# Weight loads reordered around the write of the rows, and the first expert pair's rows selected on TensorE from SBUF

## The reference

```python
h = h + hier_moe(rmsnorm(h))                       # 32 experts in 4 groups, 2 experts per token
h = h + sigmoid(rmsnorm(h) @ W_g) * (p @ W_p)      # "ple"

def hier_moe(t):
    # group by softmax, then the two best of its 8 experts; gates (token, 32), two of them not 0
    h1 = einsum('td,edf->tef', t, w_gate)          # 1024 -> 256, per expert
    h2 = einsum('td,edf->tef', t, w_up)
    a  = silu(h1) * h2 * gates[:, :, None]
    return einsum('tef,efd->td', a, w_down)        # 256 -> 1024, per expert
```

## Time and profile before

| | us |
|---|---|
| median of 3 runs | 1132.73 |
| lowest and highest run | 1126.98, 1135.36 |
| the profiled execution | 1129.97 |
| its span in the trace | 1128.3 |

### The profile page before, as it was taken

The page is one execution under the profiler, slowest core; times in us unless marked ns, Lnnn a source line. Parts: engine busy times, 40 slices in busy tenths (PEclk is TensorE's granted clock), DMA queues, the critical chain, the costliest instruction groups (busy, mean ns, idle before and its releaser), DMA issues.

```text
span 1128.3 us, 13602 instructions
## 1 busy us (share of the span) xinstructions
PE 1037.9 (92%) x5168; PEld 645.2 (57%) x5168; DVE 368.3 (33%) x941; ACT 191.1 (17%) x393; POOL 124.4 (11%) x170
## 2 busy tenths in 40 slices
PE   7999997999998788999999999999989999877893
PEld 5767665444433335777777777777654444333372
DVE  4555224222222013632236444221432222121154
ACT  2123123111111012221112010001211111111121
POOL 2443001111111101000000000000021111110101
PEclk9999998899999999999999999999969999999997
DMA  9956948699999978933334322343669999999511
GB/s 361 362 151 213 413 190 319 245 421 420 422 419 424 420 321 315 372 112 129 133 112 148 105 99 98 114 140 142 248 248 417 421 420 419 424 421 390 196 82 42
DMA packets 61475, 305.99 MB, mean 271 GB/s; under 512 B 13762, under 2 KB 21154, under 8 KB 29538
## 3 DMA queue, kind: packets, MB, share of 16 engines
q1 hardware_dynamic: 44064, 273.46, 60.8%
q0 software_dynamic: 14656, 25.72, 6.8%
q10 hardware_dynamic: 2690, 5.93, 1.4%
HBM read 308.10 MB, written 21.08 MB: 292 GB/s over the span
## 4 chain that ended last, share of the span: by engine, by line
PE 63%; DMA 22%; issue 7%; POOLq 3%; POOL 2%; DVE 2%; ACT 1%; SPq 0%; ACTq 0%; DVEq 0%
PE ps L1684 17%; DMA ring_sb<-stream 13%; PE ps L1536 13%; PE ps L1732 8%; PE ps L1545 6%; DMA scr_sb<-stream 5%; PE ps L1617 3%; PE ps L1446 3%; DMA hn_rows<-scr_sb 2%; PE ps L1522 2%; POOLq L486 2%; PE ps L1488 2%; DMA scr_sb<-hn_rows,scr_sb 1%; POOL ring_sb L487 1%; PE ps L1633 1%
## 5 line engine op out<-in xcount | busy, mean ns | idle before, releaser
L1684 PE MATMUL ps<-hn_sb,ring_sb 128*128 128x288 f32 x768 | 195.0, 408 | 0.0
L1536 PE MATMUL ps<-ring_sb,scr_sb 128*64 128x512 f32 x704 | 166.0, 621 | 26.3 <-DMA ring_sb<-stream 26.3
L1684 PEld LDWEIGHTS ps<-hn_sb,ring_sb 128*128 128x128 f32 x768 | 142.6, 190 | 37.3 <-DVE hn_sb L749 0.3
L1536 PEld LDWEIGHTS ps<-ring_sb,scr_sb 128*64 128x64 f32 x704 | 54.5, 143 | 133.9 <-issue 133.8
L1050 DVE SCALAR_TENSOR_TENSOR scr_sb<-ps,scr_sb 128x256 f32<-128x256 f32 x32 | 15.5, 484 | 254.7 <-ACT scr_sb L643 254.7
L1732 PE MATMUL ps<-scr_sb,ring_sb 128*128 128x288 f32 x384 | 95.3, 407 | 0.0
L1545 PE MATMUL ps<-ring_sb,scr_sb 128*64 128x512 f32 x352 | 85.5, 620 | 1.1 <-ACT scr_sb L647 0.9
L1732 PEld LDWEIGHTS ps<-scr_sb,ring_sb 128*128 128x128 f32 x384 | 72.2, 190 | 19.4
L1536 PE MATMUL ps<-scr_sb 128*64 128x512 f32 x240 | 73.0, 609 | 2.5 <-DMA scr_sb<-stream 2.5
L1617 PE MATMUL ps<-scr_sb,ring_sb 128*128 128x288 f32 x256 | 64.3, 406 | 0.0
L1138 DVE TENSOR_TENSOR scr_sb<-ps,std_rstd_sb 128x288 f32<-128x288 f32 x48 | 21.8, 453 | 124.4 <-PE ps L1684 124.4
(11 more groups left out here) (276 smaller groups left out, 1227.5 us busy)
## 6 DMA issues: line engine op xcount, KB each, us to landing
ring_sb<-stream SPq DMA_DIRECT2D x188, 1024.0 KB, 14.7
scr_sb<-stream SPq DMA_DIRECT2D x50, 1024.0 KB, 26.6
hn_sb<-stream SPq DMA_DIRECT2D x10, 1024.0 KB, 27.4
ring_sb<-row_pages POOLq DMA_DIRECT2D x64, 128.0 KB, 5.0
scr_sb<-key_pages SPq DMA_DIRECT2D x24, 192.0 KB, 9.1
ring_sb<-key_pages SPq DMA_DIRECT2D x24, 192.0 KB, 5.8
scr_sb<-y_rows POOLq DMA_DIRECT2D x8, 512.0 KB, 6.1
hn_rows<-scr_sb ACTq DMA_DIRECT2D x4, 512.0 KB, 10.0
```

The source lines that it names most:

```text
L1536: last = mm(ps[64 * a:64 * a + 64, 2 + b, :], xT[:, k, 64 * a:64 * a + 64], slot(a + 2 * (k // 4))[:, (k % 4) * 512:(k % 4) * 512 + 512], ...
L1684: last = mm(bank((i + 1) % 4, T), ring(s, (i % 2) * D + k * P, P), hn_t[:, k, :], start=(k == 0), stop=(k == KD - 1))
```

## The change

1. The side places are taken by the slots with n mod 18 in 8, 9, 10, 15, 16, 17. So the loads to places 12 to 14 are issued after the eighth slot of the layer, before four further loads to the ring, and not after the twelfth.
2. The load to place 15 (n = 15) waits until the rows have been written (`hn_rows`). The load to place 16 (n = 16) waits until the first pair's rows have been selected (`x_ps`, 1) and the gather of pair 1 has landed (`x_got_1`, 16). The one to place 17 waits for `member` and `rank_ps`, as before.
3. Pair 0 is not gathered. VectorE makes `m01` for pair 0 with `both(0)` right after the first `members`, and TensorE computes the transposed rows as products of `hn_tok` with `m01`: 8 column blocks x 3 token tiles, into the same PSUM banks. A float32 product is two instructions, so they are 48; they take the place of the eight transposes of `x_turn(0)`.
4. On TensorE `keep_busy(0, 1)` is gone, and `project(6, KD)` stands in its place, ahead of the first `list_pair`. `list_pair(2)` stands behind the products, `list_pair(3)` behind the first `gate_up`, and `list_pair(4)` behind the first `a_turn`.
5. On VectorE `copy_x(1)` comes before the second `take_list`; the third list goes behind `times_up` of pair 0, and the rows of the tail (`row_tail`, eight small instructions) behind `times_up` of pair 4.

```diff
+SIDE_AT = [8, 9, 10, 15, 16, 17]
...
     for L in range(2):
-        for n in range(RING, 90):
-            if n % 18 >= RING:
-                side[S_PROJ[L] + n] = n % 18
+        for n in range(90):
+            if n % 18 in SIDE_AT:
+                side[S_PROJ[L] + n] = RING + SIDE_AT.index(n % 18)
...
-        for s in range(RING, 2 * RING):
+        for s in range(RING, N_SLOTS):
             if s == RING + ROW_POS[5]:
                 sp.wait_ge(sem("rows_free"), 8)
-            load_slot(s)
-        for s in range(2 * RING, N_SLOTS):
             for L in range(2):
-                if s == S_PROJ[L] + 12:
+                if s == S_PROJ[L] + SIDE_AT[0]:
                     if L == 0:
                         sp.wait_ge(sem("key_free"), 8)
                     else:
                         sp.wait_ge(sem("g_sb"), FT)
                         sp.wait_ge(sem("vs_ps"), 1)
-                if s == S_PROJ[L] + 15:
-                    sp.wait_ge(sem("hr_ps"), 2 * L + 2)
-                if s == S_PROJ[L] + 16:
+                if s == S_PROJ[L] + SIDE_AT[3]:
                     sp.wait_ge(sem("hn_rows"), 48 * (L + 1))
+                if s == S_PROJ[L] + SIDE_AT[4]:
+                    sp.wait_ge(sem(f"x_ps{L}"), 1)
+                    sp.wait_ge(sem(f"x_got{L}_1"), 16)
+                if s == S_PROJ[L] + SIDE_AT[5]:
                     sp.wait_ge(sem(f"member{L}"), 1)
                     sp.wait_ge(sem("rank_ps"), 2 * L + 2)
...
-            for c in range(3):
+            for c in range(1, 3):
                 gather(c)
...
             members(0)
+            both(0)
             take_list(slots[:, 0, :], gr[:, 0, :], 1)
+            dve.wait_ge(sem("m01"), 2 * L + 1)
             members(1)
-            take_list(slots[:, 1, :], gr[:, 1, :], 2)
-            members(2)
             dve.wait_ge(sem("rank_ps"), 2 * L + 2)
             link(nc.vector.tensor_reduce(cmx, ps[:, 6, 0:32], AX.X, ALU.max))
             nc.vector.tensor_copy(cnt_i[:, L:L + 1], cmx).then_inc(sem("cnt"), 1)
+            copy_x(1)
+            take_list(slots[:, 1, :], gr[:, 1, :], 2)
+            members(2)
...
-            copy_x(1)
-            take_list(slots[:, 2, :], gr[:, 2, :], 3)
-            members(3)
...
             for n in range(PAIRS):
                 times_up(n + 1, n % 2, gr[:, n, :])
+                if n == 0:
+                    take_list(slots[:, 2, :], gr[:, 2, :], 3)
+                    members(3)
...
-            keep_busy(0, 1)
+            project(6, KD)
+            pe.drain().then_inc(sem("slot_free"), 1)
 
             pe.wait_ge(sem("sel_tv"), 4 * L + 4)
             list_pair(1, None)
-            project(6, 7)
+            pe.wait_ge(sem("m01"), 2 * L + 1)
+            for k in range(KD):
+                for t, (t0, tn) in enumerate(TOK):
+                    last = mm(ps[:, k // 4, (k % 4) * P:(k % 4) * P + P], hn_tok[0:tn, t, k * P:k * P + P], m01[0:tn, t, :],
+                              start=(t == 0), stop=(t == 2))
+            last.then_inc(sem(f"x_ps{L}"), 1)
             list_pair(2, 1)
-            project(7, KD)
-            pe.drain().then_inc(sem("slot_free"), 1)
             pe.wait_ge(sem("prj"), 8 * L + KD)
...
-            pe.wait_ge(sem(f"x_got{L}_0"), 16)
-            x_turn(0)
-            list_pair(3, 2)
             for n in range(PAIRS):
...
                 last.then_inc(sem(f"h_ps{L}"), 1)
+                if n == 0:
+                    list_pair(3, 2)
                 if n + 1 < PAIRS:
-                    pe.wait_ge(sem(f"x_got{L}_{(n + 1) % 2}"), 16 * ((n + 1) // 2 + 1))
+                    pe.wait_ge(sem(f"x_got{L}_{(n + 1) % 2}"), 16 * (n // 2 + 1))
                     x_turn((n + 1) % 2)
...
                 a_turn()
-                if n + 3 < PAIRS:
+                if n == 0:
+                    list_pair(4, 3)
+                elif n + 3 < PAIRS:
                     list_part(2, 5).then_inc(sem(f"list_ps{L}"), 1)
```

23 lines of the change are left out of this document (12 added, 11 removed).

## The result

| | before | after |
|---|---|---|
| median of 20 runs each | 1131.76 | 1137.03 |
| lowest and highest run | 1126.98, 1135.36 | 1129.63, 1143.92 |
| the profiled execution | 1129.97 | 1135.79 |
| its span in the trace | 1128.3 | 1134.1 |

The ratio of after to before is 1.0052, with a 95% interval of 1.0034 to 1.0071: the change makes the kernel slower by 0.5%. The time lies in the stated range, and the case "within 1%" came true, but the forecast was 0.7 us faster (1132 against the 1132.73 of then), and the kernel is 5.3 us slower. The difference of the two spans, 5.8 us, is what has to be found in the trace.

The account below looks back on a forecast made before the run. The gapless weight stream was taken to bound the expert parts. Full clock gave -2.4 - 0.6 + 1.0 = -2.0 us, partly low clock +1.6; taken -0.5 on 1132.73, forecast 1132 us, range 1124 to 1143.

Parts of the forecast that it names:

- within 1%: Whole kernel: the time differs from before by no more than about 1%, chance 0.76.
- The end of the expert part is the time from which the stream runs without a gap, plus all that is left to move: Expert parts of both layers: an earlier TensorE start helps only as much as the gapless weight loads restart earlier.
- The stream starts again with n = 16 and not with n = 19 ... even at 202.5 and 830.5: SP's loads, both layers: three more slots, 7.5 us, remain; predicted restart at 200.1 and 829.9 gains 2.4 and 0.6 us.
- I take the middle of the two near cases: TensorE's clock: between not falling (-2.0 us) and low for a part (+1.6), taken as -0.5 us.
- for a part of the products: TensorE's products: 14 of 48 at low clock, 1.3 us per layer, slower first list in layer 1; sum +1.6 us.
- low throughout: First rival, TensorE's products: half clock makes them 11.6 to 14.6 us, kernel 1142 to 1148 us; chance 0.2.
- 48 x 0.152 = 7.3 us: TensorE's products for pair 0: 48 instructions at 0.152 us each, priced from row L1707, take 7.3 us per layer.
- the full-clock case: Clock not falling during the products: restart gains of 2.4 and 0.6 us less 1.0 for gather 2, -2.0 us.
- The other reordered lists ... TensorE is ahead of the stream there: 0: Moved lists and `row_tail` on TensorE: delay of a microsecond at most, cost 0, or 1 us without that cover.
- Rival 2: First `gate_up`: TensorE's earlier start counts, saving 18 us for 1114 us; chance 0.08.
- Rival 3: Gather of pair 1 stays slow (7.9 us) or early loads do nothing: +9, about 1141 us; chance 0.05.
- one question: Asked of each edit: how much earlier does it make the load stream start again?.

Follow-up runs that it names:

- experiment 5: Kernel after, but the load to place 16 waits for the second signal on `x_ps` instead of the first: 1154.8 us, ratio 1.0204 to the kernel before.
- 1: Kernel after, but the load to place 16 waits only for the products, not for the gather of pair 1: 1130.18 us, ratio 0.9994 to before.
- 3: Kernel before with the new order of the loads alone, pair 0 gathered as before: 1120.76 us, ratio 0.9891.
- 9: Kernel after with pair 0 gathered again, no SP wait for products; load to place 16 waits for the gather of pair 0: 1118.8 us, ratio 0.9886.
- experiment 2: Kernel after with `keep_busy(0, 2)`, two unread wide products, between `project` and the first list: 1134.76 us, ratio 1.0026 to before.
- experiment 4: Kernel after with the old order of the side loads, place 16 still waiting for products and gather: 1137.2 us, ratio 1.0032 to before.
- experiment 7: Kernel after, load to place 16 waiting for the products alone, plus `keep_busy(0, 2)` behind `project`: 1127.9 us, ratio 0.9963 to before.
- experiment 10: Kernel before with the new load order, the load to place 16 waiting for the gather of pair 0: 1116.04 us, ratio 0.9853.
- experiment 12: experiment 10 with the third and fourth list, third `take_list` and `row_tail` where the change puts them: 1119.36 us, ratio 0.9902 to before.

## Why the prediction was wrong

- **"The end of the expert part is the time from which the stream runs without a gap, plus all that is left to move"**: right. A later restart alone made the kernel slower (experiment 5), an earlier one alone faster (1), one that came with an earlier TensorE faster too (3, 9), and in the profile after the lateness at the restart of layer 0 (5.5 us) is most of the lateness at its end (6.2 without what came in).
- **"The stream starts again with n = 16 and not with n = 19 ... even at 202.5 and 830.5"**: right to about 1 us: layer 1 restarted 0.2 late and gave 1.3 us back by the end; layer 0 restarted 5.5 late and was 6.4 long. In experiment 2 layer 0 restarted at 202.19, even, and its time to the next rank products was 812.33 - 181.07 = 631.3 us, 1.4 long.
- **"I take the middle of the two near cases"**: this is the step that failed. I had the clock either at full or low "for a part of the products", and gave low throughout a chance of 0.2, since only 9.5 of 16.5 us had been busy before while the products would leave no gap. In the profiled execution the clock fell in layer 0 within the first microsecond of the products and stayed at half to their end, without a gap on TensorE; in layer 1 it stayed at 1.00 until they were over. Six kernels have the products (after and experiments 1, 2, 4, 5, 7), and their traces show twelve layers: in seven the 48 instructions take 8.5 us, in five 13.2 to 14.4. The part that I had priced, 14 of 48 at the low clock, was seen in none, and its middle with the full clock is a time that no layer has. The reason against the rival, that work without a wait would keep the clock up, rested on no row; in all five slow layers the clock fell while TensorE was at work on the products. (The sum had a slip as well: the middle of -2.0 and +1.6 is -0.2 and not -0.5. It leaves the sign of the forecast as it was.) The rival's own working held: 14.4 us was its dearer end (14.6), the list 2.29 (2.13), the restart 205.2 at 11.6 us of products or 208.2 at the dearer end, plus the 0.7 that came in; measured 208.72.
- **"48 x 0.152 = 7.3 us"**: mis-sized. At full clock it is 8.4 to 8.5 us, 0.177 each: 1.2 per layer, 2.4 in all, which is more than the 2.0 us that the full-clock case was to gain. The row behind it was four instructions in 0.61 us, too few to price forty-eight. The Trainium skill's rule ("TensorE: Matmul & The Clock Gate", section "LDWEIGHTS (loading the stationary operand)"), by which they would have been an estimated 5.1 us, lies further off on the same side.
- **"The other reordered lists ... TensorE is ahead of the stream there: 0"**: not so in the first pair, where the stream waits for the places that TensorE frees. Put on top of experiment 10 the moved lists cost some 3 us (experiment 12). In the kernel after itself, where the stream starts again with n = 16 and has three more slots to move meanwhile, this is not seen: its layer 1 restarted even and ended 1.3 us early, with the same lists.
- Together: full clock in both layers was -2.0 in the prediction; with 2.4 us more for the products it is +0.4, and experiment 2 and the runs at high clocks have it between -0.5 and +1.3. The low clock adds 6.9 us for each layer that has it, and two such layers, 13.8, are the size of the 14.3 us between the lowest and the highest run. How many layers a run has is known only from traces: 0.985 with none (experiment 2), 0.976 with one, 0.969 with both (experiment 4). The median run of the kernel after lies at 0.975 to 0.976, so it is most likely one with one such layer: +6 to +8, against 5.3 measured.
- **The write "4 to 6 us"**: 2.6 to 3.9, better than thought, and worth nothing there, as said. **The gather of pair 1 "3.3"**: 3.4. **`m01` by 186.5**: 187.35, level with the list. **`gate_up` of pair 0 at about 195**: 204.05, nearly all by the clock.
- **Rival 2, TensorE's start counts (1114)**: fell. In layer 1 `gate_up` starts 15.2 us behind the rank products instead of 20.5, 5.3 us earlier, and 1.3 us came through. **Rival 3** fell too: the early loads do what they say, and by themselves are worth 1.1% (experiment 3).

The prediction put its one question to the change as a whole; it never asked what the loads' new order is worth without the products. The row of the gather of pair 0, 7.9 us on shared DMA engines against 3.3 on idle ones, was there to be read as a gain of 4.6 us that needs no products at all. With the order, the wait for that gather and everything else as before, the kernel takes 1116.0 us, with the longer `keep_busy` 1113.9: 1.5% faster than before, 2% faster than the change.

## What to carry to other kernels

When an edit makes the load queue wait for a product of the compute engine, its whole price is on the path: work out the compute at both levels of the clock, and if the two lie on both sides of even, don't take the middle: here each layer had the one or the other. Before replacing a slow small transfer by compute, look at what is queued ahead of it: holding the bulk loads back until it had landed took this kernel from 1127.7 to 1118.8 us. And when a small step is moved, follow what it releases, not only the engine on which it runs.

## What the runs showed of the hardware that I had not expected

- The clock fell during dense work, and 20 us of such work went by before it came back. In layer 0 of the kernel after it was 1.00 up to 188 us, the 48 instructions on 128x128 began at 187.4, and from 188 to 204 us it was 0.51 with TensorE busy for 16.00 of 16.00 us; it was at full again only from 208.7 us, in `gate_up`. The same instructions, after the same 0.55 us of idle time, ran at 1.00 in layer 1. The Trainium skill ("TensorE: Matmul & The Clock Gate", section "Part 1: The HAM clock gate") ties the clock to how busy TensorE has been, and this trace has a case in which being busy did not bring it back.
- The clock differs from execution to execution of one program: the same kernel takes 1128.5 or 1146.1 us (experiment 4), and two wide products on constants (four instructions) ahead of the list narrowed the spread in experiment 2 (6.2 us) but not in experiment 7 (12.8 us). What decides it in a given run was not found.
- A gather of one pair's rows lands after 3.3 or 3.4 us on idle DMA engines, 7.8 with three loads of 1 MB issued 2 us before it, and 7.7 to 10.2 us in the full stream (experiment 12, where the first two took 9.5 and 10.2). The parts of the write of the rows, 1.18 MB in all, land after 2.6 to 3.9 us with the engines nearly to themselves (after) and 8.1 to 12.5 us beside 4 MB of weights (before).
- A product of 128x128 by 128x128 in float32 costs 0.175 to 0.177 us per instruction in a row of 48 at full clock and 0.30 at the low one, a factor of 1.7 and not 2.
